# The block sums of MLP down: from GpSimd to VectorE, in five portions behind the lo parts

## The reference, cut to what matters

```python
def squared_relu_mlp(h, w_up, w_down):
    return jnp.square(jax.nn.relu(h @ w_up)) @ w_down

h = rmsnorm(x, norm_mlp[i])
x = x + squared_relu_mlp(h, w_up[i], w_down[i])      # w_up 1024x4096, w_down 4096x1024
```

## Time and profile before

| | us |
|---|---|
| median of three runs | 2612.03 (2609.56 to 2612.41) |
| profiled execution, its own time | 2612.87 |
| its span, from first to last instruction | 2611.1 |
| VectorE busy in the span | 1824.0 |
| GpSimd busy in the span | 651.1 |
| stretch of the 21 products, layer 0 | 254.61 |
| stretch of the 21 products, layer 1 | 253.27 |

### The profile page before, as it was taken

How to read it: one execution, slowest core, us unless ns; L and a number is a source line. 1 busy time by engine, 2 the same in 40 slices (tenths; PEclk the granted TensorE clock), 3 DMA queues, 4 the chain that set the end, 5 groups by cost and what they waited for, 6 DMA issues and landing times. The chain is left out here.

```text
span 2611.1 us, 35173 instructions
## 1 busy us (share of the span) xinstructions
PE 2510.6 (96%) x11641; PEld 2095.4 (80%) x11641; DVE 1824.0 (70%) x2959; ACT 999.8 (38%) x1804; POOL 651.1 (25%) x763
## 2 busy tenths in 40 slices
PE   8999999999999999999899988999999999989999
PEld 6888888878788888888677777888977888868777
DVE  6545454454577966666899878878878666678995
ACT  6232232223311544442333345555555444323332
POOL 2102011020000300000765354444440000055660
PEclk9999999999999999999999999999999999999999
DMA  6012120120333342346222111001023323723303
GB/s 206 31 49 73 48 66 25 49 73 19 144 113 97 105 149 94 108 144 247 94 83 97 45 35 41 18 25 41 17 73 126 125 96 109 260 95 125 113 1 97
DMA packets 173273, 232.00 MB, mean 89 GB/s; under 512 B 20913, under 2 KB 103121, under 8 KB 173138
## 3 DMA queue, kind: packets, MB, share of 16 engines
q1 hardware_dynamic: 170834, 226.10, 25.9%
q10 hardware_dynamic: 2304, 4.20, 0.4%
HBM read 171.53 MB, written 58.73 MB: 88 GB/s over the span
## 5 line engine op out<-in xcount | busy, mean ns | idle before, releaser
L524 PE MATMUL ps<-bh,uw_hi 128*128 128x512 f32 x880 | 343.3, 390 | 4.9 <-DVE uw_lo L792 2.3
L525 PE MATMUL ps<-bl,uw_hi 128*128 128x512 f32 x880 | 343.1, 390 | 0.0
L526 PE MATMUL ps<-bh,uw_lo 128*128 128x512 f32 x880 | 343.0, 390 | 0.0
L524 PE MATMUL ps<-opB_hi,opA_hi 128*128 128x512 f32 x672 | 267.3, 398 | 36.7 <-DVE opB_lo L1302 36.7
L703 DVE TENSOR_TENSOR xT<-ps,xT 128x512 f32<-128x512 f32 x320 | 217.2, 687 | 109.2 <-PE ps L526 108.8
L525 PE MATMUL ps<-opB_lo,opA_hi 128*128 128x512 f32 x672 | 265.7, 395 | 0.0
L526 PE MATMUL ps<-opB_hi,opA_lo 128*128 128x512 f32 x672 | 265.0, 394 | 0.0
L524 PE MATMUL ps<-aT_hi,wd_hi 128*128 128x512 f32 x640 | 254.1, 397 | 4.1 <-DVE wd_lo L474 4.1
L526 PE MATMUL ps<-aT_hi,wd_lo 128*128 128x512 f32 x640 | 250.7, 392 | 0.0
L525 PE MATMUL ps<-aT_lo,wd_hi 128*128 128x512 f32 x640 | 250.5, 391 | 0.0
L1351 POOL TENSOR_TENSOR blkAV<-blkA 128x1024 f32<-128x1024 f32 x12 | 34.5, 2876 | 781.9 <-DMA blkB<-a_dram 694.9
(11 more groups left out here) (311 smaller groups left out, 6059.4 us busy)
## 6 DMA issues: line engine op xcount, KB each, us to landing
raw<-in_w_up SPq DMA_DIRECT2D x64, 512.0 KB, 5.7
raw<-in_ret_w_in SPq DMA_DIRECT2D x48, 512.0 KB, 4.9
blkA<-in_w_down SPq DMA_DIRECT2D x24, 1024.0 KB, 5.0
blkB<-a_dram SPq DMA_DIRECT2D x24, 1024.0 KB, 7.1
a_dram<-upost SPq DMA_DIRECT2D x64, 256.0 KB, 2.1
a_dram<-xn SPq DMA_DIRECT2D x64, 256.0 KB, 2.0
xT<-x_dram SPq DMA_DIRECT2D x24, 512.0 KB, 6.1
y_dram<-xn SPq DMA_DIRECT2D x32, 256.0 KB, 2.3
```

The costliest lines, as they stand in the source:

```text
L524: pe.matmul(bank, ah, bh, start=(begin and i == 0), stop=False, skip_group_check=not begin)
L525: pe.matmul(bank, ah, bl, start=False, stop=False, skip_group_check=not begin)
L526: last = pe.matmul(bank, al, bh, start=False, stop=(i == len(pairs) - 1), skip_group_check=not begin)
```

## The change

The list `POOL_SIDES` and the function `down_pool` go, with its two calls. In their place a table `SUM_AT` says behind which product's lo pieces VectorE makes which sums, and `down_dve` calls `blk_one`, which is unchanged with all its waits, with VectorE as the engine.

```diff
-POOL_SIDES = "AB"
+SUM_AT = {0: ((1, "A"), (1, "B")), 1: ((2, "B"), (2, "A")), 2: ((3, "B"), (3, "A")), 3: ((4, "A"),), 4: ((4, "B"),)}
...
-        def down_pool(pool, layer):
-            for b in range(BLOCKS):
-                for v in (1, 2, 3, 4):
-                    for h in range(PARTS):
-                        for side in POOL_SIDES:
-                            blk_one(pool, layer, b, side, v, h)
...
                     w()
                     if i == len(todo) // 2 - 1:
                         op_add_dve(dve, layer, n, 0)
+                for v, side in SUM_AT.get(n % 7, ()):
+                    for h in range(PARTS):
+                        blk_one(dve, layer, n // 7, side, v, h)
                 for m in range(1, 4):
                     op_add_dve(dve, layer, n, m)
...
             norm_pool(pool, 1, 1)
-            down_pool(pool, 0)
             pool.wait_ge(down_mm, TILES * (DG_SW - 1))
...
             norm_pool(pool, 3, 1)
-            down_pool(pool, 1)
```

## The result

| | before | changed |
|---|---|---|
| median of four runs, us | 2612.22 (2609.56 to 2613.03) | 2574.37 (2572.59 to 2574.84) |
| profiled execution, us | 2612.87 | 2574.84 |
| its span, us | 2611.1 | 2573.0 |
| stretch of the 21 products, layer 0 | 254.61 | 234.95 |
| stretch of the 21 products, layer 1 | 253.27 | 235.26 |

A forecast was written before the change was run, and what follows sets the result against it. TensorE's waits for lo parts, with low clock behind some, bound the kernel; 18.8 us won in layer 0 and 17.3 in layer 1, together 36.1, take 2612.87 to 2576.8; said 2576.5, own range 2571 to 2583.

The forecast's parts named there:

- What bounded the kernel: In each layer's 21 MLP down products, TensorE's waits for lo parts and low clock lose 26.2 and 24.9 us.
- GpSimd's sums as the cause: Lo pieces take 3.41 us beside a GpSimd sum, 1.22 otherwise; rival of another cause: over 2680 us, within a shared 0.04.
- The price of 2.25 us: Theory for the experiments: a GpSimd two-operand addition holds up VectorE's two-operand instruction beside it by about 2.25 us.
- A sum on VectorE at 1.135 us: Each of 48 sums per layer costs VectorE 1.135 us, like a lo piece; rival of dearer sums, 2595 us: 0.07.
- upper bound of 1.28: Highest price of a VectorE sum, from an operation with float32 result taking 1.278 us; total then 2578.5 us.
- the flush rule: On VectorE, a pipeline flush behind each operation: 2.17 us a sum, 2651 us in all; slower rivals together 0.04.
- No wait in blocks 1 and 2: In steady state TensorE never waits in blocks 1 and 2, up to 1.29 us a sum.
- The spare of 1.25 us: At product 2's tile 1 in blocks 1 and 2, the tightest place, VectorE's add has 1.25 us to spare.
- The start of a layer: Block 0, products 1 and 2: TensorE late by 3.4, 0.6 and 2.4 us in layer 0, 6.6 in all in layer 1.
- The clock allowance: Behind the last wait at a layer's start, low clock costs up to 1.9 us; half taken, 1.0 a layer.
- Waits and clock in the loss before: In the two stretches before the change, loss exceeds the listed waits by 14.5 us, all put down to the clock.
- Transfers and SyncE's order: Transfers don't slow lo pieces; on SyncE, B11 and A11 wait for sums but are needed three products later or more.

The follow-up runs named there:

- e1: Changed kernel plus 48 unused two-operand additions of 128x1024 per layer on GpSimd, which nothing waits for until the products are through: 2722.92 us.
- e2: Changed kernel plus 48 unused memsets of 128x1024 per layer on GpSimd, which write SBUF and read nothing: 2572.49 us.
- e5: Changed kernel plus one unused 128x1024 addition on VectorE behind the sums of step 1 of every block: 2578.05 us.
- e6: Changed kernel plus one unused 128x1024 addition on VectorE behind the sums of each of steps 0, 1 and 2 of every block: 2584.63 us.
- e4: Changed kernel with tile arrival semaphores shared otherwise: A12 with B21, A22 and B22 each alone, instead of A12 with B22 and A22 with B21: 2558.60 us.
- e3: Changed kernel with side B's four sums back on GpSimd and side A's four kept on VectorE: 2614.15 us.
- e10: Changed kernel with v3 and v4 of side B back on GpSimd, 4 of 16 sums a block: 2602.32 us.

## Why the prediction was right

- **What bounded the kernel**: TensorE's waits for lo parts in the two stretches. Of the 38.1 us of the span, 37.7 came from there.
- **GpSimd's sums as the cause**: shown by the lo pieces, 144 us shorter without them, and by e1, where additions that feed nobody bring the slow pieces back; e2 says what in them does it. The price of 2.25 us holds where both engines run such instructions without a pause. Over the whole kernel before, the lo pieces took 143 us more than at 1.22 for 96 sums, 1.5 us each.
- **A sum on VectorE at 1.135 us**: 1.135 measured. The upper bound of 1.28 wasn't touched. By the flush rule of "VectorE: DVE Perf Modes" in the Trainium skill, section "The DRAIN you can't avoid", a sum would have cost 2.17 us, an estimate, and the time would have been 2651. The trace doesn't agree for these instructions: 1.135 us from start to start.
- **No wait in blocks 1 and 2**: none. The spare of 1.25 us was found by e5 and e6.
- **The start of a layer**: worked out as product 1 late by 3.4 us, then 0.6 and 2.4. Layer 1, counted in the same way from the times at which the starts were due, shows 3.6, 0.6 and 2.4. Layer 0 shows 3.3, no second wait, and 1.2: a low-clock phase of some eight matmuls in product 1, behind the first wait, took the place of the rest. The tile that ends it starts at 1266.11, where I had VectorE's add visible at 1266.2. The 0.15 us allowed for a signal was too much: TensorE starts 0.05 us behind VectorE's end.
- **The clock allowance** of 1.0 us a layer is the one term that was clearly mis-sized. It was 0 in both, since no phase followed the last wait. So the stretches lost 6.6 and 6.9 us, not 7.4 and 7.6, which is 1.5 of the 2.0 us between the 2576.8 forecast for the profiled execution and its 2574.8.
- **Waits and clock in the loss before**: the prediction put all of the 14.5 us by which the loss exceeds the listed waits down to the clock. Layer 1 of the changed kernel lost 6.9 us with 5.8 of listed waits and no matmul at the lower clock, so each of its three waits costs some 0.3 us more than the list says: the list counts from the modelled end of the matmul before, 0.16 us behind the usual spacing, and the matmul after the first comes 0.33 us later instead of 0.23. At the 14 waits of the kernel before that is some 4 us, an estimate, and the six phases of low clock there cost some 10 us together. The forecast wasn't touched by it, since it goes by the length of the stretches.
- **Transfers and SyncE's order**: nothing became late. In the changed kernel no wait stands in blocks 1 and 2, and in e4 none in the whole of both stretches.

Two things that I had not worked out were shown only behind it: that half of the sums on GpSimd would save nothing (e3), and that the place of the last waits was one semaphore shared by an early and a late tile (e4). The prediction took the late start as given.

## What to carry to other kernels

Before giving VectorE's work to GpSimd, look at the operands. When two-operand additions in SBUF run on both, VectorE's instruction of 1.22 us grew to 3.4 here, so handing over 16 of them a block held VectorE for longer than making them would (143 us against 109). Price such work at the place where it falls, by the slack of the instruction that TensorE waits for, and not by an average over a block: with four of the sums on GpSimd the kernel took 28 us more, with two others, made where VectorE had time to spare, no more. And when a last wait stays at one place, look at what its semaphore counts besides what is needed.

## What the runs showed of the hardware

- A GpSimd memset of 128x1024 float32 (0.96 us) beside VectorE costs VectorE nothing (e2). A GpSimd addition with both operands in SBUF, 2.39 us when nothing holds it up, takes VectorE's two-operand instruction from 1.22 to 3.4 us and itself grows to 3.2 or 3.3 (e1). An add of VectorE with one operand in PSUM stays at 0.68 beside either. Once, VectorE's two sums ran unhindered and GpSimd's took 4.38 us (e10); no run here shows what decides which of the two is held.
- TensorE's clock fell to its lower level behind a wait of 3.12 us in layer 0 of the changed kernel and not behind one of 3.47 in layer 1. The windows behind the two waits show a granted clock (last column but two) of 0.50 and of 1.00:

```profile
1251.00:1254.30 3.30, 3.30 (x9) 2.60 (x8) 3.30 (x4) 2.15 (x3) 0.00 (x0) 0.50 0.00 0
2297.30:2308.00 10.70, 10.70 (x47) 8.86 (x48) 10.70 (x12) 4.02 (x4) 0.00 (x0) 1.00 0.28 100
```

In the kernel before it fell behind one wait of 2.12 us and not behind another. The length of the wait alone doesn't decide, and no run here shows what does. Such a phase costs 1.5 to 2.0 us, and nothing where VectorE sets the next start.
